# Moving the gate projection of layer A under the threshold search, and the late modulation under the mask stage

## What is computed

```python
c_act = jax.nn.silu(c)
for i in range(DEPTH):                              # two layers
    mod = (c_act @ mod_w[i] + mod_b[i])[:, None, :] # shift, scale, res_gate, 1024 each
    h = rms_norm(x, pre_g[i]) * (1.0 + scale) + shift
    # mixer A:
    proj = h @ w_in                                 # 256 + 128 + 64 + 8 narrow columns, then 1024 gate columns
    c_q, c_kv, k_idx, w_idx = ...                   # the narrow columns, the first three normalised
    gate = proj[..., o4:]
    q_abs = ...(c_q @ w_uq, w_uk)
    score = sum_h w_idx * relu(q_idx . k_idx);  _, sel = lax.top_k(score, k_top)
    ...
    y = (o * jax.nn.silu(gate)) @ w_out
    x = x + res_gate * rms_norm(y, post_g[i])
```

## Time and profile before

| what | time |
|---|---|
| three timed runs | 4289.83, 4300.61, 4303.97 us; median 4300.61 |
| the profiled execution | 4292.6 us |
| its span, first to last instruction | 4290.8 us |
| TensorE's granted clock, mean | 0.906 of full |
| busy over the span | PE 82%, DVE 49%, ACT 48%, POOL 12% |

### The profile page before, as it was taken

One profiled execution on the slowest core, in us unless ns is written; L12 is line 12 of the kernel. 1 busy time (PEld: TensorE's weight loads), 2 busy tenths in 40 slices (PEclk: granted clock), 3 DMA queues, 4 the chain that ended last, 5 costly groups with the idle time before them and its releaser, 6 DMA issues. The chain is left out here.

```text
span 4290.8 us, 64366 instructions
## 1 busy us (share of the span) xinstructions
PE 3502.0 (82%) x18498; PEld 2627.5 (61%) x18498; DVE 2117.6 (49%) x5809; ACT 2040.5 (48%) x3499; POOL 524.7 (12%) x560
## 2 busy tenths in 40 slices
PE   5598577764049999999969499999988888899699
PEld 5487455653036666666658478888975555555587
DVE  0401288999955555555556500000017777777344
ACT  0412267988447777777722401111126666666322
POOL 0011000551001111111101011111100000000011
PEclk9898898865569999999989799999999999999789
DMA  5222533872012222222245222222221111110343
GB/s 121 99 67 65 173 70 123 227 211 80 27 52 82 77 77 76 76 74 75 65 165 176 98 76 71 73 71 71 69 76 46 43 43 47 43 48 29 120 132 113
DMA packets 361723, 378.40 MB, mean 88 GB/s; under 512 B 71792, under 2 KB 291344, under 8 KB 359952
## 3 DMA queue, kind: packets, MB, share of 16 engines
q1 hardware_dynamic: 361488, 375.35, 29.5%
HBM read 237.89 MB, written 137.36 MB: 87 GB/s over the span
## 5 line engine op out<-in xcount | busy, mean ns | idle before, releaser
L1002 DVE CUSTOM_DVE_ANT_0 a_att_sb_lg<-a_att_ps_s,mask 128x512 f32<-128x512 f32 (+3 forms) x512 | 302.7, 595 | 283.3 <-PE a_att_ps_s L896 240.3
L895 PE MATMUL a_att_ps_s<-a_att_sb_k,a_att_sb_q 128*128 128x512 f32 (+3 forms) x640 | 291.3, 455 | 169.9 <-DMA a_att_sb_k<-scratch_kT 153.5
L1076 ACT ACTIVATE a_att_sb_pT<-a_att_ps_t 128x512 f32<-128x512 f32 (+3 forms) x640 | 317.0, 530 | 146.6 <-PE a_att_ps_t L912 138.7
L494 ACT ACTIVATE b_qkgv_sb_o_lo<-b_qkgv_ps_acc 128x512 f32<-128x512 f32 x128 | 76.6, 598 | 637.7 <-PE b_qkgv_ps_acc L477 472.6
L912 PE MATMUL a_att_ps_t<-ident,a_att_sb_lg 128*128 128x128 f32 x2176 | 345.5, 282 | 38.6 <-issue 29.4
L1068 ACT ACTIVATE b_att_sb_lg<-b_att_sb_lg,b_att_sb_negm 128x384 f32<-128x384 f32 (+15 forms) x256 | 305.7, 1199 | 110.9 <-DVE b_att_sb_negm L1010 110.1
L1004 DVE TENSOR_SCALAR_CACHE_REDUCE b_att_sb_lg<-b_att_ps_s 128x512 f32<-128x512 f32 (+3 forms) x512 | 289.7, 591 | 137.4 <-PE b_att_ps_s L901 131.4
L1033 DVE MEMSET b_att_sb_mx<- 128x256 f32 x1 | 0.3, 272 | 721.8 <-PEq L88 721.8
L1068 ACT ACTIVATE a_att_sb_lg<-a_att_sb_lg,a_att_sb_negm 128x384 f32<-128x384 f32 (+15 forms) x256 | 307.4, 1201 | 81.6 <-DVE a_att_sb_negm L1010 81.6
L912 PEld LDWEIGHTS a_att_ps_t<-ident,a_att_sb_lg 128*128 128x128 f32 x2176 | 252.0, 142 | 148.7 <-issue 100.4
L901 PE MATMUL b_att_ps_s<-b_att_sb_k,b_att_sb_q 64*128 64x512 f32 (+3 forms) x1280 | 323.2, 592 | 14.0 <-DMA b_att_sb_k<-scratch_kT 9.9
(11 more groups left out here) (273 smaller groups left out, 7135.1 us busy)
## 6 DMA issues: line engine op xcount, KB each, us to landing
select_sb_mod_w<-in_mod_w SPq DMA_DIRECT2D x16, 1024.0 KB, 7.1
a_att_sb_q<-scratch_qT SPq DMA_DIRECT2D x128, 128.0 KB
a_att_sb_q<-scratch_qT SPq DMA_DIRECT2D x256, 64.0 KB
a_att_sb_k<-scratch_kT SPq DMA_DIRECT2D x64, 256.0 KB
b_qkgv_sb_w<-in_b_w_in SPq DMA_DIRECT2D x32, 512.0 KB
mod_sb_w<-in_mod_w SPq DMA_DIRECT2D x4, 2048.0 KB, 8.7
scratch_gateT<-a_gate_sb_o_lo SPq DMA_DIRECT2D x32, 256.0 KB, 2.4
scratch_qT<-select_sb_o_hi SPq DMA_DIRECT2D x32, 256.0 KB, 3.4
```

The source lines that it names most:

```text
L895: nc.tensor.matmul(out, q[:, p // 2 % QS, 0, cols], k[:, slot, a:z], start=True, stop=False)
L1002: x = nc.vector.tensor_tensor_reduce(out, src, tab, 1.0, 2 * NEG, ALU.add, ALU.max, top[:, col:col + 1])
L1076: nc.scalar.activation(pT[:, r % 2, a:z, c:c + P], t_ps[:, n % TR, 0:z - a], ACT.Copy).then_inc(t_left, 1)
```

## The change

The gate's stage is taken out. `stage_input` stores each block h of layer A to a new scratch tensor `hT_dram` (32 stores of 256 KB), from a ring of four buffers in place of two. In select, each pass now has four tiles: one gate tile and the next three small ones. A gate tile is 8 matmuls of 128x512 in the full format, from plain weights (512 KB loaded for each tile, two buffers) and the 8 blocks h of one group of 512 tokens (loaded back for each group, 8 passes long). ACT leaves the gate tile with SiLU behind its second count. `RA` becomes 8 and `RO` 3. The late modulation (16 halves, loads, gate rows, columns) moves to the mask stage, on PE and SP; DVE takes the gate rows behind the eleventh block and the columns at the end. The core of the diff:

```diff
@@ stage_input
-        h = st.sb("h", [P, 2, 512], F32)
+        h = st.sb("h", [P, 4, 512], F32)
+        h_stored = [st.sem(f"h_stored{u}") for u in range(4)]
 sync, step(g, u, last), behind load(g + 2, u):
+                if h_dram is not None:
+                    for k in range(KD):
+                        sp.wait_ge(scaled, g * KD + k + 2)
+                        sp.sem_inc(idle_sp, 1)
+                        sp.dma_start(h_dram[k * P:(k + 1) * P, ds(g * 512, 512)], h[:, k % 4]).then_inc(h_stored[k % 4], 16)
 scalar:
-                    nc.scalar.activation(h[:, k % 2], pt[:, k], ACT.Identity, ...)
+                    if h_dram is not None:
+                        act.wait_ge(h_stored[k % 4], 1 + 16 * (k // 4) + g * 32)
+                    nc.scalar.activation(h[:, k % 4], pt[:, k], ACT.Identity, ...)
@@ stage_select
-    TILES = [(x, kind, n, g) for x, (kind, n) in enumerate(UNITS) for g in range(8 if kind == "v" else G)]
+    SMALL_TILES = [(x, kind, n, g) for x, (kind, n) in enumerate(UNITS) for g in range(8 if kind == "v" else G)]
+    TILES = [tile for s in range(PASSES) for tile in [(None, "gate", s % KD, s // KD)] + SMALL_TILES[3 * s:3 * s + 3]]
-    RA, RO = 3, 2
+    RA, RO = 8, 3
 sync:
             load_weights(1)
-            for j in range(2):
-                load_modulation(j)
+            load_gate_weights(0)
+            for k in range(KD):
+                load_h(0, k)
+            load_gate_weights(1)
...
-                if t % EVERY == EVERY - 1 and t // EVERY + 2 < len(HALVES):
-                    sp.wait_ge(mod_used, t // EVERY + 1)
-                    load_modulation(t // EVERY + 2)
+                if t % PER_PASS == 1 and t // PER_PASS + 2 < PASSES:
+                    sp.wait_ge(multiplied, t)
+                    load_gate_weights(t // PER_PASS + 2)
+                if t % PER_PASS == 1 and t // PER_PASS % KD == KD - 2 and t // PER_PASS + 2 < PASSES:
+                    last, group = t + PER_PASS - 1, t // PER_PASS // KD
+                    for k in range(KD - 1):
+                        sp.wait_ge(h_used, group * (KD - 1) + k + 1)
+                        load_h(group + 1, k)
+                    sp.wait_ge(multiplied, last + 1)
+                    load_h(group + 1, KD - 1)
...
+                elif kind == "gate":
+                    sp.wait_ge(left, t + 1)
+                    sp.dma_start(gateT[n * P:(n + 1) * P, g * 512:(g + 1) * 512], o_plain[:, t % RO]).then_inc(stored[t % RO], 16)
 gpsimd, split_weights(x):
-                    pool.wait_ge(multiplied, FIRST[x - 1])
+                    pool.wait_ge(multiplied, UNTIL[x - 2])
 tensor:
+            def gate(t, n, g):
+                j = t // PER_PASS
+                pe.wait_ge(gate_in[j % 2], 16 * (j // 2 + 1))
+                if t >= RA:
+                    pe.wait_ge(left, t - RA + 1)
+                for k in range(KD):
+                    if n == 0:
+                        pe.wait_ge(h_in[k], 16 * (g + 1))
+                    m = nc.tensor.matmul(acc[:, t % RA], w_gate[:, j % 2, k], h[:, k], start=(k == 0), stop=(k == KD - 1))
+                    if n == KD - 1 and k < KD - 1:
+                        m.then_inc(h_used, 1)
+                m.then_inc(multiplied, 1)
...
-                if t % EVERY == EVERY - 1 and t // EVERY < len(HALVES):
-                    modulate(t // EVERY)
 scalar, leave(t):
-                    if TILES[t - RO][1] == "v":
+                    if TILES[t - RO][1] in ("q", "k"):
+                        act.wait_ge(lo_done, SPLIT_BEFORE[t - RO] + 1)
+                    else:
                         act.wait_ge(stored[t % RO], stores_until(t))
-                nc.scalar.activation(o_plain[:, t % RO], acc[:, t % RA], ACT.Copy, ...)
+                nc.scalar.activation(o_plain[:, t % RO], acc[:, t % RA], ACT.Silu if kind == "gate" else ACT.Copy, ...)
 vector:
-                if s == PASSES - 8:
-                    dve.wait_ge(mod_used, len(HALVES))
-                    dve.wait_ge(gate_in, 64)
-                    for l in range(2):
-                        nc.vector.tensor_tensor(gp[:, l], flat(pgate[:, l]), gp[:, l], ALU.add).then_inc(gate_added, 1)
-                    modulation.finish_columns(nc, dve, 1, pcol, ada, scale, columns_done)
@@ stage_mask: the modulation's loads, matmuls and POOL's multiplication as they were in select, and
+    HALVES = [(chunk, half) for chunk in (4, 5, 10, 11, 6, 7, 8, 9) for half in range(2)]
 vector, in the loop over the blocks n:
+                if n == NS - 4:
+                    dve.wait_ge(mod_used, NGATE)
+                    dve.wait_ge(gate_in, 64)
+                    for l in range(2):
+                        nc.vector.tensor_tensor(gp[:, l], flat(pgate[:, l]), gp[:, l], ALU.add).then_inc(gate_added, 1)
+            dve.wait_ge(mod_used, len(HALVES))
+            modulation.finish_columns(nc, dve, 1, pcol, ada, scale, columns_done)
@@ program
-            stage_input(nc, sems, "a_in", ins["x"][0], ada, 0, ident, hT)
-            stage_project(nc, sems, "a_gate", [Job("silu", hT, KD, lambda n: win[:, :, ds(n * P + SMALL, P)], KD, 1.0, gateT)])
+            stage_input(nc, sems, "a_in", ins["x"][0], ada, 0, ident, hT, hT_dram)
```

More of the change, by code:

```diff
@@ L282, in _ @@
             groups(sp, step)
+            if h_dram is not None:
+                for u in range(4):
+                    sp.wait_ge(h_stored[u], 1 + 2 * G * 16)
         @block.scalar
@@ L1468, in stage_mask, with _, load @@
         block = st.block()
+        @block.sync
+        def _(sp):
+            def load(j):
+                (chunk, half), (l, third, part) = HALVES[j], chunk_place(HALVES[j][0])
+                c0 = third * D + part * 512 + half * 256
+                sp.dma_start(mod_w[:, j % 2], ins["mod_w"][l].rearrange("(k p) n -> p k n", p=P)[:, :, c0:c0 + 256]).then_inc(mod_in[j % 2], 16)
+            load(0)
+            load(1)
+            for l in range(2):
+                sp.dma_start(postg[:, l], ins["post_g"][l].partition_broadcast(P)).then_inc(gate_in, 16)
+                sp.dma_start(gp[:, l], ins["mod_b"][l, 2 * D:3 * D].partition_broadcast(P)).then_inc(gate_in, 16)
+            for j in range(2, len(HALVES)):
+                sp.wait_ge(mod_used, j - 1)
+                load(j)
+            sp.wait_ge(gate_done, 2)
+            for l in range(2):
+                sp.dma_start(gp_dram[l], gp[:, l]).then_inc(gate_stored, 16)
+            sp.wait_ge(gate_stored, 32)
+        @block.tensor
+        def _(pe):
+            for j, (chunk, half) in enumerate(HALVES):
+                l, third, part = chunk_place(chunk)
+                pe.wait_ge(mod_in[j % 2], 16 * (j // 2 + 1))
+                if third < 2:
+                    for f in range(2):
+                        c = third * KD + part * 4 + half * 2 + f
+                        for k in range(KD):
+                            m = nc.tensor.matmul(pcol[:, c:c + 1], mod_w[:, j % 2, k, f * P:(f + 1) * P], modulation.cact[:, k:k + 1],
+                                                 start=(k == 0), stop=(k == KD - 1))
+                else:
+                    for k in range(KD):
+                        m = nc.tensor.matmul(pgate[:, l, part, half * 256:(half + 1) * 256], modulation.cwide[:, k], mod_w[:, j % 2, k],
+                                             start=(k == 0), stop=(k == KD - 1))
+                m.then_inc(mod_used, 1)
         @block.scalar
@@ L1873, in program @@
     qT, kT, v = scratch("qT", (2, D, T)), scratch("kT", (2, D, T)), scratch("v", (T, D))
+    hT_dram = scratch("hT", (D, T))
     gateT, oT, x1 = scratch("gateT", (D, T)), scratch("oT", (D, T)), scratch("x1", (T, D))
```

101 lines of the change are left out of this document (45 added, 56 removed).

## The result

The changed kernel takes **4086.6 us** (median of four runs, 4080.8 to 4092.3) where the kernel before took 4302.3 beside it (four runs): a ratio of 0.9507, 95% interval 0.9492 to 0.9522. The table sets the profiled executions side by side (spans 4290.8 and 4078.9 us, difference -211.9; forecast -175.5).

A forecast was written before the change was run, and what follows sets the result against it. PE was taken to bound a_gate, DVE select and mask. Terms -188.3 + 5 + 3.8 + 4 = -175.5 gave 4117.1 from the profiled execution, 4125.1 from the median; forecast 4121 us, range 4100 to 4190.

The forecast's parts named there:

- Nothing for attention: Layer A's attention, which the change doesn't touch: no term in the sum, so a forecast of 0 us.
- a_gate, -188.3: The gate's own stage: its whole stretch of 188.3 us goes, barrier and weight wait included.
- a_in, +5: Input stage: 32 more stores and ACT's waits for them cost 5 us, bounds 0 and +8.
- Select, pass 0: Search's first pass: loads of h and a cold first gate tile put its compare 11.3 us later (+9 to +16).
- Select, passes 1 to 10: Search passes with q tiles: paced by PE at 11.4 us each, 114.0 against 116.1, so -2.1 us.
- Select, passes 11 to 31: Search's last 21 passes: 10.96 us each, 230.2 against 241.6, so -11.4 us, partly because the modulation leaves.
- The +6: Select: 6 us allowed for three changes of the group of h, late stores and a clock that falls now and then.
- Mask, +4: Mask stage: PE's halves hidden, DVE's gate rows and columns 2.9 us, POOL's multiplications beside DVE 1 us.
- Table loads: Rival in select: Sign and SiLU in different tables, two loads per pass, +70 us, 4190; chance 0.10.
- PE bounds select: Rival in select: lower clock or waits for gate weights, +21 us (4142) to +71 us (4192); chance 0.13.
- ACT's 0.25 us: Rival in select: late gate stores use up ACT's last 0.25 us of room per pass, +25 us, 4146; chance 0.10.
- Slower: Rival in select: PE stays at 1.2 GHz throughout, +285 us, 4406, slower than before; chance 0.02.

The follow-up runs named there:

- e2: The changed kernel with 114 empty PE instructions behind the search's last tile: 4133.7 us, ratio 0.9617.
- e4: The changed kernel with eight buffers for h in the input stage in place of four: 4080.2 us, ratio 0.9492.
- e3: The changed kernel with the gate's tile last of a pass's four tiles, its loads moved to match: 4068.3 us, ratio 0.9463.
- e6: The kernel before with only the late modulation moved from the search to the mask, a_gate kept: 4287.1 us, ratio 0.9971.
- e11: The changed kernel, gate first, with ACT taking tiles out behind each pass's first four counts, not its last four: 4092.6 us, ratio 0.9520.

## Why the forecast missed, point by point

**Nothing for attention: the step that failed.** The sum gave the untouched stages nothing, on the ground that their work is unchanged. Their work is, their place in PE's instruction stream isn't. What the runs showed in place of that zero is -46.0 us, brought back in full by 114 empty instructions (e2). The two views that would have told are the DMA queues cut down to that stage, with 66 instruction packets in 913 us, and the gap of PE with "issue" as its releaser. They show that the kernel before already lay badly, so a shift could only leave the 46 us or give them back. If the bad places are some third of the 256, which the seven places tried suggest and don't prove, a rival of "-46 by luck" with a chance of about two thirds was due. The measured time lies under the range by this gift alone: without it, at 4133.7, it would have been inside. The Trainium skill (Runtime: NRT & Kernel Launch, "Instruction fetch mechanics") says that instructions come in blocks of 16 KiB or 256 of them; the packets agree (1.08 MB in 66). It also says that a taken branch to outside a window of two blocks forces a fetch. The measurement decides against that for this loop: it is over five blocks long, and at the good places it turns without a packet. The same section gives TensorE room for 128 KiB, eight such blocks, which the good places agree with and the bad ones, and layer B's loop, don't.

**a_gate, -188.3, right.** The stage went with nothing left behind.

**a_in, +5, measured +8.9.** The step named both waits, and priced them 0 to 3 us each; they took 3.7, and e4, without them, is 7.0 us shorter there. The store that ACT waits for is the one issued behind a 2 MB load, and the load's 7.6 us of the earlier trace rows was in view.

**Select, pass 0, right.** Forecast +11.3 for the first compare, measured +12.0 behind the score stage's end (+11.1 with the indexer and score, which were 0.9 shorter: 736.36 - 568.56 = 167.8, where the indexer's projection stands at 178.9). The reason was right too: the gate's tile begins when h has landed, below full clock, and takes 10 us.

**Select, passes 1 to 10: wrong by 7.1 us, and for a wrong reason.** I had PE pace them at 11.4 us, 114.0 in all. They took 12.1 each, 121.1, and 11.0 of the 11.5 us above 10.96 each lie in stretched short steps. In e3, with POOL off most of these steps and the same work on PE, passes 3 to 9 took 11.0 to 11.5. PE waited for gate weights (20.3 us in 13 waits) without holding a pass up: it ran far enough ahead that ACT never waited for it.

**Select, passes 11 to 31: a term that was mis-sized.** 10.96 each, 230.2 in all, was taken as the floor that is reached once the modulation is gone; it measured 238.8. In e6, where only the modulation goes, the floor is indeed reached in all but one of these passes. With the gate's tiles it is reached from 24 on; most of passes 11 to 21 took 11.3 to 11.5, and 7.0 of the 8.6 us are in the short steps. The +6 that the forecast allowed for late loads and stores covers less than half of the two misses together. The forecast knew the mechanism, from the earlier trace rows, and charged it to the modulation and to the mask alone. It didn't ask when, in a pass, POOL's other work falls. POOL's casts in select, before and after, with what ended POOL's idle time ahead of them:

```profile
L1317 POOL CAST select_sb_o_hi<-select_sb_o_plain 128x512 fp32r<-128x512 f32 x64 | 39.1, 610 | 105.0 <-DMA scratch_qT<-select_sb_o_lo 57.8 <-DMA scratch_kT<-select_sb_o_lo 34.2 <-ACT select_sb_o_plain L1381 12.8
```

```profile
L1338 POOL CAST select_sb_o_hi<-select_sb_o_plain 128x512 fp32r<-128x512 f32 x64 | 39.1, 610 | 125.0 <-ACT select_sb_o_plain L1398 111.2 <-DMA scratch_kT<-select_sb_o_lo 7.1 <-DMA scratch_qT<-select_sb_o_lo 6.5
```

With two output buffers the casts waited for stores and fell anywhere. In the changed kernel, with three, they follow ACT's leave at once, and the last leave of a pass stands next to the short steps. The number of buffers wasn't varied alone, so how much of this is theirs isn't shown.

**Mask, +4, measured +3.1: near by luck.** PE's halves ended at 1033.9 beside DVE's work that ends at 1045.5, as forecast. But POOL's two multiplications cost 3.1 us where the forecast took 1: a scan took 5.14 us in place of 3.88, and the next step 2.05 in place of 0.16, until POOL was done:

```profile
1012.14 8.26 POOL L1551 TENSOR_TENSOR mask_sb_gp<-mask_sb_gp,mask_sb_postg 128x1024 f32<-128x1024 f32 x2 [80.35 <-DVE mask_sb_gp L1633]
1018.36 2.05 DVE L1601 SCALAR_TENSOR_TENSOR mask_sb_need<-mask_sb_rank,mask_sb_size 128x1 f32<-128x1 f32 x1
```

The gate rows cost 2.4 more. What hid this is that DVE began the stage 2.2 us sooner behind the last compare, and e6, with the same mask, has that too; its cause wasn't looked for.

**The rivals.** Table loads: one load in all of select, so Sign and SiLU share a table. PE bounds select: clock 0.92, no. ACT's 0.25 us: the gate's store never took it (0.8 us in two waits); e11 did, and there were 0.14. Slower: the clock stayed up. The range's lower bound was looser than its reason: no cost in a_in and select at its low bound give 4108 from 4121, not 4100.

## What to carry to other kernels

A stage's time can move by some per cent although nothing in it changed: before a difference in an untouched loop is explained by data or heat, count its instruction packets, and try a few dozen empty instructions ahead of it. When short serial steps of one engine stand between passes, ask what the other engine on the same port starts at that very moment; moving a tile that needs no work there into the last slot cost nothing here and gave 18 us. And look at which side of an engine's last needed instruction an optional one stands: behind it the leave was free, ahead of it it cost its 0.48 us less the room of 0.14.

## What the runs showed of the hardware

- A loop of PE of 1354 instructions turned without fetching at three places in PE's stream (100, 135, 217) and fetched at four (2, 11, 75, 77), which cost 27 to 46 us over its stage, 5.3 to 7.6 us per jump back. 25 empty instructions decided it. A loop of 1393 fetched at all seven places where it lay.
- A DVE instruction on 128x14 elements, 0.17 us alone, took 0.28 to 0.62 us when it started under POOL's cast of 128x512 (0.61 us), and 1.12 to 1.29 us under POOL's subtraction (1.3 us), and each ended 0.03 us behind POOL's. That happened to `tensor_tensor` (L1438, L1451) and to `tensor_scalar` (L1449, L1454) alike. None ran its 0.17 us wholly inside an instruction of POOL.
- Empty semaphore instructions on PE cost about 0.15 us each (an estimate: 142, 183 and 192 of them put the mask's first `kept` 6.0, 12.3 and 13.7 us later). The first 60 or so are hidden, for PE ended its tiles some 10 us ahead of the last compare: 25 and 60 of them delayed nothing.
